# Linear attention output: state moved against held queries in two directions at once, norm taken with tokens on partitions, then transposed

## The reference

```python
def gla_chunked(q, k, v, logg, s0):
    ...
    b = jnp.cumsum(logg, axis=2)
    q_e = q * jnp.exp(b)
    a = jnp.einsum('bnihd,bnjhd->bnhij', q_e, k * jnp.exp(-b))
    a = jnp.where(jnp.tril(...), a, 0.0)
    o_intra = jnp.einsum('bnhij,bnjhv->bnihv', a, v)
    def step(s, xs):
        q_c, k_c, v_c, dec_c = xs
        o_c = jnp.einsum('bchd,bhdv->bchv', q_c, s)
        s = dec_c[..., None] * s + jnp.einsum('bchd,bchv->bhdv', k_c, v_c)
        return s, o_c
...
    o = o * lax.rsqrt(jnp.mean(o * o, axis=-1, keepdims=True) + EPS)
    o = o.reshape(bsz, L, GLA_VAL) * lp['gla_norm_g'] * jax.nn.silu(r)
    y_a = o @ lp['w_o_gla']
```

## Time and profile before

| | |
|---|---|
| median of 3 runs | 3516.43 us (3512.21 to 3517.94) |
| the profiled execution, its own time | 3512.08 us |
| its span, first to last instruction | 3510.4 us |
| granted TensorE clock, mean | 0.99 |
| TensorE busy | 3442.5 us, 98% |
| VectorE busy | 1236.9 us, 35% |
| ScalarE busy | 1255.6 us, 36% |
| GpSimd busy | 1471.6 us, 42% |
| stage of the four heads | about 164 to 410 us of the span |

### The profile page before, as it was taken

How to read it: one execution, slowest core, us unless ns; L and a number is a source line. 1 busy time by engine, 2 the same in 40 slices (tenths; PEclk the granted TensorE clock), 3 DMA queues, 4 the chain that set the end, 5 groups by cost and what they waited for, 6 DMA issues and landing times.

```text
span 3510.4 us, 39172 instructions
## 1 busy us (share of the span) xinstructions
PE 3442.5 (98%) x16124; PEld 2774.4 (79%) x16124; DVE 1236.9 (35%) x2137; ACT 1255.6 (36%) x1924; POOL 1471.6 (42%) x672
## 2 busy tenths in 40 slices
PE   8999999999999999999999999999999999999998
PEld 5777887887888887887777888888887778888776
DVE  3265784533111144212553111111113652111544
ACT  4524323433322332223454222322223553222544
POOL 4222444554544444445423444444445224444332
PEclk9999999999999999999999999999999999999999
DMA  7211223442333323333112223233332122223211
GB/s 269 70 51 55 90 97 111 153 150 73 126 132 120 102 96 132 135 94 108 55 34 96 99 95 95 88 105 98 94 96 88 33 76 95 97 90 102 72 60 55
DMA packets 99294, 341.19 MB, mean 97 GB/s; under 512 B 11371, under 2 KB 11755, under 8 KB 98956
## 3 DMA queue, kind: packets, MB, share of 16 engines
q1 hardware_dynamic: 98352, 336.97, 28.9%
q10 hardware_dynamic: 764, 1.72, 0.1%
HBM read 336.02 MB, written 2.10 MB: 96 GB/s over the span
## 4 chain that ended last, share of the span: by engine, by line
PE 93%; DVE 2%; ACT 2%; DMA 1%; issue 1%; POOL 1%; SPq 0%; DVEq 0%; ACTq 0%
PE ps L1183 26%; PE ps L1185 25%; PE ps L1184 25%; PE ps L1202 2%; PE ps L1204 2%; PE ps L1203 2%; PE ps L1484 2%; PE ps L1511 1%; PE ps L1497 1%; PE ps L1399 1%; PE ps L1269 1%; POOL t L2662 1%; PE ps L1413 0%; PE ps L1239 0%; DMA t<-in_w_ada 0%
## 5 line engine op out<-in xcount | busy, mean ns | idle before, releaser
L2662 POOL TENSOR_TENSOR t<-t,t 128x1024 fp32r<-128x1024 f32 (+2 forms) x588 | 1361.2, 2317 | 1925.3 <-ACT t L1579 1924.3
L1183 PE MATMUL ps<-t,t 128*128 128x512 f32 (+1 forms) x4048 | 1607.7, 397 | 17.4 <-POOL t L2662 8.6
L1185 PE MATMUL ps<-t,t 128*128 128x512 f32 (+1 forms) x4048 | 1583.9, 391 | 0.0
L1184 PE MATMUL ps<-t,t 128*128 128x512 f32 (+1 forms) x4048 | 1579.7, 390 | 0.0
L1183 PEld LDWEIGHTS ps<-t,t 128*128 128x128 f32 x4048 | 764.0, 189 | 184.8 <-issue 17.5
L1185 PEld LDWEIGHTS ps<-t,t 128*128 128x128 f32 x4048 | 763.2, 189 | 167.5
L1184 PEld LDWEIGHTS ps<-t,t 128*128 128x128 f32 x4048 | 764.1, 189 | 157.9 <-issue 1.4
L1579 ACT CAST t<-t 128x1024 fp32r<-128x1024 f32 (+2 forms) x588 | 584.3, 995 | 571.6 <-PE ps L1185 416.3
L2455 DVE TENSOR_TENSOR t<-t,ps 128x512 f32<-128x512 f32 x110 | 75.7, 688 | 531.7 <-PE ps L1185 516.9
L1648 ACT CAST t<-t 128x512 fp32r<-128x512 f32 x158 | 97.0, 621 | 401.4 <-DVE t L2455 361.5
L1835 ACT ACTIVATE t<-t 128x512 f32<-128x512 f32 x88 | 55.6, 632 | 315.1 <-DVE t L2448 315.0
(11 more groups left out here) (285 smaller groups left out, 2283.2 us busy)
## 6 DMA issues: line engine op xcount, KB each, us to landing
t<-in_w_f1i SPq DMA_DIRECT2D x88, 512.0 KB, 3.3
t<-in_w_f2i SPq DMA_DIRECT2D x88, 512.0 KB, 3.3
t<-in_w_ada SPq DMA_DIRECT2D x72, 512.0 KB, 4.4
t<-in_w_ffi SPq DMA_DIRECT2D x44, 512.0 KB, 3.7
t<-in_w_f1o SPq DMA_DIRECT2D x32, 512.0 KB, 3.6
t<-in_w_f2o SPq DMA_DIRECT2D x32, 512.0 KB, 3.5
t<-in_w_gate SPq DMA_DIRECT2D x24, 512.0 KB, 4.0
t<-in_w_out SPq DMA_DIRECT2D x48, 256.0 KB, 2.6
```

Of the source, the lines that this page charges most:

```text
L1183: e.matmul(out, wh[:, at], X.hi[c][:, 0:N], start=c == first, stop=False)
L1184: e.matmul(out, wh[:, at], X.lo[c][:, 0:N], start=False, stop=False)
L1185: m = e.matmul(out, wl[:, at], X.hi[c][:, 0:N], start=False, stop=c == final)
L2662: e.tensor_tensor(k.WL[:, n % NHL, 0:w], k.raw[:, j % NRAW, 0:w], f(k.WH[:, n % NHL, 0:w]), ALU.subtract).then_inc(*k.rest.inc(('rest', j) ...
```

## The change

The read-out holds the 64 queries of a chunk and moves the state, 256 columns. The output of direction d lies on 64 partitions of a bank, tokens on partitions: chunk c goes to partitions 64 * (c % 2), in bank v = c // 4. In each step the chunks of the two directions lie on different partition halves and in different banks, and the waits for both states stand ahead of both products. `intra` holds the masked products and moves 256 value columns. Since tokens are on partitions, the norm needs neither mean products nor row broadcasts: `chain_end` squares on ScalarE with a sum along the free axis, four times (128 tokens by 256), and takes the root. `head_scale`, one quarter later, has VectorE take the reciprocal and write both banks, scaled, to QK; this frees the banks. `head_turn` of the head before stands behind `inner` and `masked`: eight transposes, and the gain on the way out of PSUM, one half by VectorE, one by ScalarE.

```diff
@@ first @@
-        if h:
-            on.head_scale(0, h - 1)
         beside(6)
         on.inner(h)
         on.masked(h)
         if h:
-            on.head_scale(1, h - 1)
+            on.head_turn(h - 1)
...
-            if h and step == 3:
-                on.head_scale(2, h - 1)
         on.chain_end(h)
         beside(1)
+        on.head_scale(h)
...
-        if i < 3:
-            on.head_scale(i, 3)
+        if i == 0:
+            on.head_turn(3)
@@ Sync.sgu_loads @@
-        self.wait_ge('ssq', ('o', 3), 1)
+        self.wait_ge('root', ('o', 3))
@@ Tensor @@
-            for v in range(2):
-                e.matmul(self.bank('bo', h, v)[:, at], k.VT[:, t, w + v * 128:w + v * 128 + 128], k.AM[:, at], ...)
+            e.matmul(self.bank('bo', h, t // 2)[:, 256 * (t % 2):256 * (t % 2) + 256], k.AM[:, at], k.VT[:, t, w:w + 256], ...)
...
-            for v in range(2):
-                m = e.matmul(self.bank('bo', h, v)[:, at], state[:, v * 128:v * 128 + 128], k.QE[:, d, at], ...)
+            p, t = (64 * (c % 2), c // 2)
+            out = self.bank('bo', h, t // 2)[p:p + 64, 256 * (t % 2):256 * (t % 2) + 256]
+            m = e.matmul(out, k.QE[:, d, 64 * c:64 * c + 64], states[d], ...)
...
+    def head_turn(self, h):
+        k, e = (self.k, self.e)
+        for v in range(2):
+            b = self.take(k.banks, 'ot', h, v)
+            for t in range(4):
+                self.wait_ge('o rows', h, t // 2)
+                w = 256 * (t % 2) + 128 * v
+                m = e.transpose(b[:, t * 128:t * 128 + 128], k.QK[:, h, t // 2, w:w + 128], const(k, 'ident'))
@@ Scalar @@
-        e.copy(k.QK[:, h, 1, :], self.bank('bo', h, 1))
+        for t in range(4):
+            w = slice(256 * (t % 2), 256 * (t % 2) + 256)
...
+            e.activation(k.SQ[:, w], self.bank('bo', h, t // 2)[:, w], ACT.Square, accum_out=c[:, t:t + 1])
+        self.settle()
+        e.activation(c, c, ACT.Sqrt, scale=1.0 / 256, bias=unit(k, 1))
...
+    def head_turn(self, h):
+        self.wait_ge('filled', ('ot', h, 1))
+        e.activation(k.O[:, 2 * h + 1, :], self.bank('ot', h, 1), ACT.Copy, scale=param(k, 'gla_norm_g', 2 * h + 1))
@@ Vector @@
-    def chain_end(self, h):
-        e.tensor_copy(k.QK[:, h, 0, :], self.bank('bo', h, 0))
...
+    def head_scale(self, h):
+        self.wait_ge('root', ('o', h))
+        e.reciprocal(c, c)
+        self.settle()
+        for v in range(2):
...
+            e.tensor_tensor(rows, o, root, ALU.mult)
...
+    def head_turn(self, h):
+        self.wait_ge('filled', ('ot', h, 1))
+        e.tensor_scalar(k.O[:, 2 * h, :], self.bank('ot', h, 0), param(k, 'gla_norm_g', 2 * h), None, ALU.mult)
@@ Pool @@
-    def head_scale(self, s, h):
-        if s == 0:
-            self.square(head_sum(self.k, h), 1, None, None)
```

More of the change, by code:

```diff
@@ L1388, in chain @@
             self.outer(h, step + 1, d)
+        states = []
+        for d in range(2):
+            if step == 0:
+                states.append(k.SIN[:, d, h, :])
+                self.wait_ge('copied state', d, h)
+            else:
+                states.append(gla_ring(k).of(('st', h, d))[:, 256 * ((step - 1) % 2):256 * ((step - 1) % 2) + 256])
+                self.wait_ge('state', h, d, step - 1)
         for d in range(2):
             c = step if d == 0 else 7 - step
-            at = slice(64 * c, 64 * c + 64)
-            if step == 0:
-                state = k.SIN[:, d, h, :]
-                self.wait_ge('copied state', d, h)
-            else:
-                state = gla_ring(k).of(('st', h, d))[:, 256 * ((step - 1) % 2):256 * ((step - 1) % 2) + 256]
-                self.wait_ge('state', h, d, step - 1)
-            for v in range(2):
-                m = e.matmul(self.bank('bo', h, v)[:, at], state[:, v * 128:v * 128 + 128], k.QE[:, d, at], start=step == 0 and d == 0, stop=step == 7 and d == 1, skip_group_check=True)
+            p, t = (64 * (c % 2), c // 2)
+            out = self.bank('bo', h, t // 2)[p:p + 64, 256 * (t % 2):256 * (t % 2) + 256]
+            m = e.matmul(out, k.QE[:, d, 64 * c:64 * c + 64], states[d], start=step < 2, stop=step == 7, skip_group_check=True)
             m.then_inc(*k.filled.inc(('inter', h, d, step), *([('free', ('st', h, d))] if step == 7 else []), *([('filled', ('bo', h))] if step == 7 and d == 1 else [])))
@@ L1541, in head @@
             mm.then_inc(*k.filled.inc(('filled', ('hm', n)), ('free', ('head', n))))
-def head_sum(k, h):
-    sq = Sum(('o', h), k.R[h % 2], S, ('oscaled', h - 2) if h > 1 else ('normed', 'nx' if h else 'cx', 7))
-    sq.last = 1
-    sq.slots = head_square_ring
-    return sq
 def conv_sum(k):
-    return Sum('cn', k.R[1], S, ('oscaled', 3), range(8))
+    return Sum('cn', k.R[1], S, ('normed', 'nx', 7), range(8))
 def diff_sum(at, i):
@@ L1733, in chain_end @@
         k, e = (self.k, self.e)
+        c = self.take(k.cols, 'cols', ('o', h))[:, 0:4]
         self.wait_ge('filled', ('bo', h))
-        e.copy(k.QK[:, h, 1, :], self.bank('bo', h, 1)).then_inc(*k.act.inc(('o', h, 1), ('free', ('bo', h, 1))))
+        for t in range(4):
+            w = slice(256 * (t % 2), 256 * (t % 2) + 256)
+            if t == 0 and h == 0:
+                self.wait_ge('filled', ('state', 1, 3))
+            if t > 1:
+                self.wait_ge('o square', h, t - 2)
+            e.activation(k.SQ[:, w], self.bank('bo', h, t // 2)[:, w], ACT.Square, accum_out=c[:, t:t + 1]).then_inc(*k.act.inc(('o square', h, t)))
+        self.settle()
+        e.activation(c, c, ACT.Sqrt, scale=1.0 / 256, bias=unit(k, 1)).then_inc(*k.act.inc(('root', ('o', h))))
     def conv_gate(self, i):
@@ L1742, in conv_gate @@
         e.activation(k.HC[:, i % 6, :], self.bank('c2', i), ACT.Sigmoid).then_inc(*k.act.inc(('conv gate', i), ('free', ('c2', i))))
-    def head_scale(self, s, h):
-        k, sq = (self.k, head_sum(self.k, h))
-        if s == 0:
-            for v in range(2):
-                self.square(sq, v, k.O[:, 2 * h + v, :], ('o', h, v))
-        if s == 1:
-            self.roots(sq, 1, 4.0)
-        if s == 2:
-            self.row(sq)
+    def head_turn(self, h):
+        k, e = (self.k, self.e)
+        self.wait_ge('filled', ('ot', h, 1))
+        e.activation(k.O[:, 2 * h + 1, :], self.bank('ot', h, 1), ACT.Copy, scale=param(k, 'gla_norm_g', 2 * h + 1)).then_inc(*k.act.inc(('o scaled', 2 * h + 1), ('free', ('ot', h, 1))))
     def gla_out(self, i):
@@ L2006, in conv_ring @@
     return ring(k, 'conv', k.tmp[0:3], [('inter', 3, 1, 7)])
-def head_square_ring(k):
-    return ring(k, 'head squares', [k.SQ], [('filled', ('state', 1, 3))])
 def row_ring(k):
@@ L2300, in conv_in @@
         self.conved += 1
[L2302 to L2310 removed]
+    def head_scale(self, h):
+        k, e, c = (self.k, self.e, self.k.cols.of(('cols', ('o', h)))[:, 0:4])
+        self.wait_ge('root', ('o', h))
+        e.reciprocal(c, c).then_inc(*k.dve.inc())
+        self.settle()
+        for v in range(2):
+            rows, o = (ap.rearrange('p (a n) -> p a n', a=2) for ap in (k.QK[:, h, v, :], self.bank('bo', h, v)))
+            root = c[:, 2 * v:2 * v + 2].rearrange('p (a n) -> p a n', n=1).broadcast_to([128, 2, 256])
+            e.tensor_tensor(rows, o, root, ALU.mult).then_inc(*k.dve.inc(('o rows', h, v), ('free', ('bo', h, v)), *([('free', ('cols', ('o', h)))] if v else [])))
+    def head_turn(self, h):
+        k, e = (self.k, self.e)
+        self.wait_ge('filled', ('ot', h, 1))
+        e.tensor_scalar(k.O[:, 2 * h, :], self.bank('ot', h, 0), param(k, 'gla_norm_g', 2 * h), None, ALU.mult).then_inc(*k.dve.inc(('o scaled', 2 * h), ('free', ('ot', h, 0))))
     def gla_out(self, i):
```

26 lines of the change are left out of this document (4 added, 22 removed).

## The result

| | before | changed |
|---|---|---|
| median, runs of the same chip | 3516.6 us (3512.21 to 3517.94, 4 runs) | 3496.86 us (3494.91 to 3500.81, 4 runs) |
| ratio, with its 95% interval | | 0.9953 [0.9938, 0.9968] |
| the profiled execution, its own time | 3512.08 us | 3496.82 us |
| its span | 3510.4 us | 3494.8 us |

The change makes the kernel faster. The forecast was 3501.6 us with 14.8 us of gain. The ratio says 16.5 us (11 to 22), the medians of four runs each lie 19.7 us apart, the two profiled executions 15.3.

The account below looks back on a forecast made before the run. TensorE, busy 98% of the span, was taken as the bound. Terms -8.6 - 0.2 - 6.7 + 3.5 - 5.4 + 0.65 + 2.0 sum to -14.8 us: 3497.3 against the profiled execution, 3501.6 against the median; range 3493 to 3511.

Parts of the forecast that it names:

- state products: Read-out in each chunk step: a pair takes 0.59 us against 0.92 for the old eight records; 8.6 us less.
- intra-chunk products: Products inside the chunks: 16 records of 128 columns become 8 of 256; 0.2 us less over four heads.
- mean products and row broadcasts removed: Norm on TensorE: four mean products and four row broadcasts per head go; 6.7 us less over four heads.
- transposes: Eight added per head in the place of the mean products, at 0.11 us each; 3.5 us more.
- the wait in step 4 of heads 1 to 3: Second outer product waits for state updates queued behind VectorE's scalings; the wait goes, 5.4 us less.
- the two waits that stay: Head 2, step 2, and a smaller one in head 3: TensorE's saving there is waited for; 0.65 us more.
- bank wait in heads 1 and 3: Output banks, before the next head's second triangular product: free at F + 4.7, needed at F + 5.0; no wait.
- the stop after head 1: Value projection waits for logs delayed by ScalarE's longer norm chain; 2.0 us more, bounds 1.5 to 3.7.
- reading of rows 5: Trace rows of L1217 and L1511: products on different partition groups run together, so a step's pair takes 0.59 us.
- third rival: The 5.4 us wait only moves, as head_turn's new scaling and the taps take its place: 3507.0 us; chance 0.06.
- fourth rival: The longer stop after head 1 also costs clock: gain 13.1 to 11 us, up to 3505.5 us; chance 0.07.
- slower rival: Every chunk step waits for both directions' states, VectorE setting the pace: 42 us added, about 3544 us; chance 0.04.

Follow-up runs that it names:

- leave-out run: Changed kernel with the norm's squares and root left out, ScalarE copying four columns instead (output not normed): 3493.32 us, ratio 0.9949.
- first run with both edits: Changed kernel with head 1's logarithms split three and one (fourth behind the second value-projection quarter) and VectorE's states ahead of conv input: 3491.12 us, ratio 0.9947.
- repeat with both edits: Changed kernel with logarithms split three and one and states ahead of conv input, timed again in five rounds beside the changed kernel: 3492.84 us, ratio 0.9939.

## Why the prediction was right

| step of the prediction | forecast, us | measured, us |
|---|---|---|
| state products | -8.6 | -8.2 (24 x 0.305 and 8 x 0.11) |
| intra-chunk products | -0.2 | -0.3 (0.075, four times) |
| mean products and row broadcasts removed | -6.7 | -7.2 (0.90, eight times) |
| transposes | +3.5 | +3.6 (0.79 and 0.10 behind them, four times) |
| the wait in step 4 of heads 1 to 3 | -5.4 | -5.4 (1.84, 1.81, 1.79) |
| the two waits that stay | +0.65 | +0.7 (idle 0.67 and 0.57) |
| bank wait in heads 1 and 3 | 0 | 0 |
| the stop after head 1 | +2.0 | +2.8 |
| sum | -14.8 | -13.94 for the stage |

Each size is read from the projection products of the two traces, matched one by one: how much shorter the stretch around the place has become, the product behind it included. The mean products of heads 0 to 2 cannot be read alone, since the transposes stand in their very place; there the difference is under 0.01 us, and head 3, where both stand apart, gives 0.90 for the one and 0.90 for the other. The measured sizes sum to -14.0; the stage gives -13.94. So three terms were mis-sized, and they partly cancel: the state products by 0.4 us, the removed products by 0.5 the other way (a group was counted at 0.81 to 0.87, and 0.90 came out with what the product behind it gives back), the stop by 0.8. That the sum lies within 0.9 us of the stage is in part owed to this.

*The pair of state products.* The reading of rows 5, that passes of different halves run together also for this shape and into two banks, was the step on which most hung; the run with both on one half shows it: 0.42 us a step, 13.5 us in all. The overhead beyond the two passes, 0.16 us, was right to the hundredth: 0.59 against 2 x 0.213. The Trainium skill (TensorEngine Tiling (Array Packing), Key Properties) says that a change of the tiling mode drains TensorE. The trace does not contradict it, but the 0.16 us hold the first load and the drain together, and no run parts the two. Only the way back to full width costs 0.02 that I had rounded down: 0.4 us of the sum.

*The wait that goes.* Right in cause and size. The kernel before with the scaling moved lost its waits and 5.44 us, so it was the scaling in VectorE's queue and not the number of TensorE's products. The third rival (it only moves) did not come true.

*The stop after head 1* is the term that was mis-sized most, +2.0 for +2.8, inside its bounds of 1.5 to 3.7. Two errors went against each other. The chain was overpriced: a square with its accumulator read has a pitch of 0.36 us here, not the 0.47 of the place that I read it from (L1872, an exponential with a bias per partition), so the root ends at 255.49, 3.2 us after the banks are full and not 3.5, and the four Abs take 2.06 us, not 2.3. From ScalarE's first instruction behind the full banks (252.31; 259.05 before) to the first product behind the stop it is 13.36 us against 12.00, 1.36 more. But the half clock, which I had put into the upper bound and into the fourth rival, did fall behind the wait; it costs 1.5 us there. 1.36 and 1.5 are the 2.8. The leave-out run parts them in the same way, 1.19 and 1.6.

*The output banks* are scaled out earlier than forecast: VectorE starts on the first at 210.75 us and is through with both at 212.04, while TensorE asks at 212.27, 5.0 us after they were full. The forecast had that 5.0 right, although the terms that it names (12 projection products, 4 transposes, 16 records) sum to 5.2.

*The slower rival.* Had each step waited for both states, TensorE's waits would stand in 28 steps; there are two, and both are older than the change. In both, VectorE takes in a conv tile (L2289) ahead of the states, and putting the states first removed them.

*From the stage to the whole.* The sum was for the profiled execution, 3497.3, and 3496.82 came out. That is closer than the terms deserve: the stage gave 0.9 us less than forecast and the rest 1.3 us more. Read by the windows of the kernel before (busy times, then the clock), two half-clock stretches stand where the changed kernel had full clock:

```profile
1329.50:1332.90 3.40, 2.80 (x7) 2.25 (x8) 3.40 (x2) 0.53 (x1) 3.09 (x2) 0.50 0.00 0
1882.50:1885.90 3.40, 3.40 (x8) 2.71 (x9) 1.01 (x2) 1.05 (x2) 2.27 (x1) 0.50 0.47 154
```

and the changed kernel has a longer one of its own where the kernel before has 3.4 us:

```profile
801.90:808.70 6.80, 5.76 (x14) 4.50 (x15) 1.45 (x2) 2.77 (x4) 4.02 (x2) 0.50 0.41 140
```

The matched products step by -1.5, -1.6 and +1.1 us at these places, and the changed kernel reaches the first matched product 0.35 us later: with the stage that makes the 15.6 us between the spans. Such stretches change from execution to execution of one and the same kernel, and so I take them for scatter, not for an effect of the change. The time on record, 3496.86, lies 4.7 under the forecast of 3501.6 for the same reason: the forecast carried the 4.3 us by which the profiled execution of before lay under its median, and the changed kernel's lay on its own.

## What to carry to other kernels

Where small products pay for loading 128 weight columns and not for what is moved, holding the small side and moving the large one pays only if the halves of the array are filled side by side: here the same instructions with both outputs on one half gave nothing. An operation that waits for a far-off result should not stand in an engine's queue ahead of what the bound engine needs next; moving such a call, without any new arithmetic, gave 5.4 us in one kernel and 1.3 in the other. And when a stop is cured by moving work later, read who is queued behind the moved work: one placement gave nothing, the other, one quarter earlier, 3.75 us.

## What was not expected of the hardware

The stretches at half clock last from 3.4 to 10.2 us in these traces. One of 3.4 us costs 1.5 to 1.6 us of TensorE's work where TensorE is busy, nothing where it lies ahead of a stop, and 0.9 where TensorE without it would wait for GpSimd (at 134.8 us of the kernel before). They come and go between executions of the same kernel. The changed kernel's three profiles agree on the stage to 0.05 us, and their spans are 3494.8, 3491.9 and 3496.9. The start alone, up to the first projection product, moved the profiles by up to 4 us against each other.

What TensorE did before the clock fell behind head 1 was not the same each time. With stops of 3.90 us (five profiles: three of the changed kernel, one each with the states first and with the transposes twice) and with the one of 3.85 (both directions on one side) it fell every time, from 0.2 us before the stop's end to 1.1 us behind it. With stops of 2.71 us (without the root) and 2.61 us (scaling moved) it did not fall, but with the one of 2.42 us (logarithms later) it did, 0.5 us behind it. So the length of the stop alone does not decide it. It also fell without any stop, 0.5 to 0.7 us behind the 33-row products of the logarithms: behind sixteen records in the kernel before (264.6 us), and behind twelve in the kernels with the logarithms later (263.9), with the fourth one earlier (266.0) and in the first run with both edits (262.1). In the repeat with both edits, and behind the sixteen records of the changed kernel and of the one with the scaling moved, it did not. What sets them apart is left open.
